# Plain fp32 router logits, fourteen weight cells of the first item fetched earlier, and sum products two down slots earlier

## What is computed

```
logits = tok @ router                       # 256 x 8, tok = rms_norm(h) * gain
top_v, top_i = top_k(logits, 2)
w = softmax(top_v)
out = sum_e gates[:, e] * ((silu(tok @ w_gate[e]) * (tok @ w_up[e])) @ w_down[e])
h = h + out;  return rms_norm(h, final_norm)
```

## Time and profile before

| | |
|---|---|
| median of three runs | 1258.49 us |
| profiled execution, span | 1259.62 us, 1257.8 us |
| PE, PEld busy | 1234.0, 872.8 us |
| DVE, ACT, POOL busy | 641.3, 562.0, 99.8 us |
| transfers | 424.48 MB, mean 337 GB/s |
| attention and dense parts | 0 to 437 us |
| first item's products | from 447 us |
| last product of an item | ends at 1248.2 us |

### The profile page before, as it was taken

The page is one execution under the profiler, slowest core; times in us unless marked ns, Lnnn a source line. Parts: engine busy times, 40 slices in busy tenths (PEclk is TensorE's granted clock), DMA queues, the critical chain, the costliest instruction groups (busy, mean ns, idle before and its releaser), DMA issues.

```text
span 1257.8 us, 18674 instructions
## 1 busy us (share of the span) xinstructions
PE 1234.0 (98%) x7266; PEld 872.8 (69%) x7266; DVE 641.3 (51%) x788; ACT 562.0 (45%) x895; POOL 99.8 (8%) x260
## 2 busy tenths in 40 slices
PE   9998999999999999999999999999999999999887
PEld 8988999999999954487575457848447765733232
DVE  5787765555765400288383257838126855620011
ACT  6565454443655421388173158527027835500001
POOL 1000000000000074100001200000210000021000
PEclk9999999999999999999999999999999999999999
DMA  9933545357632299999999999999999999999997
GB/s 329 378 136 135 182 167 188 134 166 234 228 118 100 96 426 428 422 424 427 426 426 427 424 425 426 425 426 425 428 422 426 427 407 418 424 429 424 427 427 291
DMA packets 72136, 424.48 MB, mean 337 GB/s; under 512 B 5457, under 2 KB 24050, under 8 KB 48242
## 3 DMA queue, kind: packets, MB, share of 16 engines
q1 hardware_dynamic: 71696, 422.76, 83.0%
q10 hardware_dynamic: 354, 0.54, 0.1%
HBM read 422.23 MB, written 1.05 MB: 337 GB/s over the span
## 4 chain that ended last, share of the span: by engine, by line
PE 89%; DMA 5%; ACT 2%; DVE 2%; issue 1%; POOLq 0%; POOL 0%; ACTq 0%; DVEq 0%; SPq 0%
PE psB L2100 10%; PE psY L2115 9%; PE psA L2100 7%; PE psY L1725 7%; PE psY L1727 7%; PE psY L1726 7%; PE psB L1725 6%; PE psA L1725 5%; PE psB L1727 5%; PE psB L1726 5%; PE psA L1727 5%; PE psA L1726 5%; DMA ring<-in_moe_w_up 2%; DMA ring<-in_moe_w_down 2%; PE psY L2066 1%; PE psY L1873 1%
## 5 line engine op out<-in xcount | busy, mean ns | idle before, releaser
L1585 DVE TENSOR_TENSOR wlo<-ring,whi 128x2048 fp32r<-128x2048 f32 (+3 forms) x171 | 289.1, 1727 | 150.7 <-ACT whi L950 148.5
L950 ACT CAST whi<-ring 128x1024 fp32r<-128x1024 f32 (+1 forms) x276 | 259.5, 981 | 155.1 <-DMA ring<-in_moe_w_down 72.4
L1332 DVE TENSOR_TENSOR wlo<-ring,whi 128x1024 fp32r<-128x1024 f32 (+2 forms) x104 | 152.3, 1485 | 17.6 <-ACT whi L764 17.5
L764 ACT CAST whi<-ring 128x1024 fp32r<-128x1024 f32 (+1 forms) x134 | 133.4, 1023 | 60.0 <-PE psY L1727 28.3
L2100 PE MATMUL psB<-ring,resT 128*64 128x512 f32 x620 | 149.0, 598 | 7.4 <-DMA ring<-in_moe_w_up 5.4
L2100 PE MATMUL psA<-ring,resT 128*64 128x512 f32 (+1 forms) x624 | 113.9, 486 | 0.0
L1725 PE MATMUL psA<-xhi,whi 128*128 128x256 f32 x368 | 105.0, 285 | 2.6 <-DVE wlo L1332 1.2
L2100 PEld LDWEIGHTS psA<-ring,resT 128*64 128x64 f32 x624 | 44.8, 137 | 89.1 <-issue 89.1
L1725 PE MATMUL psB<-xhi,whi 128*128 128x256 f32 x368 | 106.4, 289 | 0.0
L1726 PE MATMUL psA<-xlo,whi 128*128 128x256 f32 x368 | 102.7, 279 | 0.0
L1726 PE MATMUL psB<-xlo,whi 128*128 128x256 f32 x368 | 102.7, 279 | 0.0
(11 more groups left out here) (382 smaller groups left out, 2147.1 us busy)
## 6 DMA issues: line engine op xcount, KB each, us to landing
ring<-in_moe_w_down SPq DMA_DIRECT2D x50, 2048.0 KB, 15.6
ring<-in_moe_w_up SPq DMA_DIRECT2D x53, 1792.0 KB, 18.1
ring<-in_moe_w_gate SPq DMA_DIRECT2D x50, 1792.0 KB, 14.9
ring<-in_moe_w_gate SPq DMA_DIRECT2D x13, 1024.0 KB, 15.5
ring<-in_ffn_w_gate SPq DMA_DIRECT2D x5, 2048.0 KB, 8.8
ring<-in_ffn_w_up SPq DMA_DIRECT2D x5, 2048.0 KB, 7.8
ring<-in_ffn_w_down SPq DMA_DIRECT2D x5, 2048.0 KB, 8.0
ring<-in_moe_w_gate SPq DMA_DIRECT2D x13, 768.0 KB, 14.0
```

The source lines that it names most:

```text
L764: nc.scalar.copy(hi_of(m, size), part_of(ring, s, g, size)).then_inc(hi_done, size)
L950: nc.scalar.copy(hi_of(NG + m, size), item_part(ring, m, size)).then_inc(hi_done, size)
L1332: nc.vector.tensor_tensor(part_of(wlo, s, g, size), part_of(ring, s, g, size), f(hi_of(m, size)), ALU.subtract).then_inc(lo_done, size)
L1585: nc.vector.tensor_tensor(item_part(wlo, m, size), item_part(ring, m, size), f(hi_of(NG + m, size)), ALU.subtract).then_inc(lo_done, size)
```

## The change

The logits are multiplied in plain fp32 from `resT` (stationary, 128 x 128) with the 8 router columns moving, straight into 128 tokens x 8; the rounded parts, their copy and the summing products go. `ahead[1]` now takes the first eight spare cells, `ahead[0]` the next eight. Gate 6 of the first item is split in six cells, which wait for NG - 8 used cells only, and its last cell, which waits for NG. Between them SP waits for the last weighing of values and issues up 0 and the first cell of up 1 (eight cells). In the loop's item three down slots come in pieces, and the sums' products stand before down 1, 2 and 3 instead of 3, 4 and 5.

```diff
-    SUM_AT = {item_slot["up", 7]: (0, 1), item_slot["down", 3]: (1, 1), item_slot["down", 4]: (0, 0), item_slot["down", 5]: (1, 0)}
+    SUM_AT = {item_slot["up", 7]: (0, 1), item_slot["down", 1]: (1, 0), item_slot["down", 2]: (0, 0), item_slot["down", 3]: (1, 1)}
+    IN_PIECES = 3
...
+                last_dense = isinstance(i, int) and i == 0 and x == CELLS - GS
-                if runs and runs[-1][0] == what and runs[-1][1] + runs[-1][2] == at:
+                if runs and runs[-1][0] == what and runs[-1][1] + runs[-1][2] == at and not last_dense:
...
-            return [([ring_all, ahead[0], ahead[1]][what][:, at * W:(at + n) * W], q, n) for what, at, n, q in runs]
-        def few_used(j):
-            end = item_from[j] + item_cells[j]
+            return [([ring_all, ahead[1], ahead[0]][what][:, at * W:(at + n) * W], q, n) for what, at, n, q in runs]
+        def first_used(j, q, n):
+            end = item_from[j] + q + n
             if end <= CELLS:
                 return NG - CELLS + -(-end // GS) * GS
             return NG + max(end - CELLS - AHEAD_CELLS if end < 2 * CELLS + AHEAD_CELLS else end - CELLS, 0)
...
-                    if first:
-                        sp.wait_ge(group_used, few_used(j))
-                        if item_from[j] <= CELLS + GS < item_from[j] + item_cells[j]:
-                            sp.wait_ge(logit_mm, 1)
...
+                            if first and early_ahead(j, q):
+                                continue
+                            if first and item_from[j] + q == CELLS - GS:
+                                sp.wait_ge(pv_done, 2 * UNITS)
+                                first_rows(item_slot["up", 0], 0)
+                                first_rows(item_slot["up", 1], 0)
+                            if first:
+                                sp.wait_ge(group_used, first_used(j, q, n))
                             sp.dma_start(to, w[0][e, at * P:(at + 1) * P, q * W:(q + n) * W]).then_inc(item_full[j], 16)
...
-                    if not isinstance(i, int) and j >= FS - 2:
+                    if not isinstance(i, int) and j >= FS - IN_PIECES:
...
             split_to(NG)
-            for q in range(2):
-                act.wait_ge(block_added, 2 * q + 2)
-                raw_hi(2 * q, 2)
-            act.wait_ge(block_added, 6)
-            raw_hi(4, 2)
-            for k in range(6, KD):
-                act.wait_ge(block_added, k + 1)
-                raw_hi(k, 1)
             row_square(0, 0)
-            act.wait_ge(logit_mm, 1)
-            nc.scalar.copy(logitT[:, :], psA[0:2 * E, 0, 0:T]).then_inc(logitT_out, 1)
...
-            for q in range(2):
-                raw_lo(2 * q, 2)
...
-            dve.wait_ge(logit_mm, 2)
+            dve.wait_ge(logit_mm, 1)
...
-                    pe.wait_ge(tlo_done, k + 1)
-                    for which in (0, 1):
-                        ins = mm(psA[0:2 * E, 0, 0:T], rt_parts[:, k, :], T_part(which, k, 1),
-                                 start=k == 0 and which == 0, stop=k == KD - 1 and which == 1)
+                    pe.wait_ge(block_added, max(k + 1, 4))
+                    for tb in range(TB):
+                        ins = mm(psA[:, 1, tb * E:(tb + 1) * E], resT[:, k, tb * P:(tb + 1) * P], rt[:, k, :],
+                                 start=k == tb == 0, stop=k == KD - 1, skip_group_check=True)
...
-            pe.wait_ge(scales_set, 3)
-            pe.wait_ge(logitT_out, 1)
-            for tb in range(TB):
-                ins = mm(psA[:, 1, tb * E:(tb + 1) * E], logitT[:, tb * P:(tb + 1) * P], sum_parts[:, :], start=True, stop=True)
-            ins.then_inc(logit_mm, 1)
```

More of the change, by code:

```diff
@@ L273, in trunk @@
         pickT = sb("pickT", [P, T], F32R)
-        sum_parts = sb("sum_parts", [2 * E, E])
         rs_of_slot = sb("rs_of_slot", [P, 1])
         ident_r = sb("ident_r", [P, P], F32R)
-        rt_parts = sb("rt_parts", [P, KD, 2 * E], F32R)
         top = sb("top", [P, TB, E])
         top_at = sb("top_at", [P, TB, E], U32)
-        logitT = sb("logitT", [2 * E, T])
         count = pickT[:, :].rearrange("p (a t) -> p a t", a=2)
@@ L332, in trunk @@
         first_full = [[sem(f"first_full{j}_{a}") for a in range(len(FIRST_PARTS[j]) - 1)] for j in range(2)]
-        piece_full = [[sem(f"piece_full{a}_{k}") for k in range(FBW - 1)] for a in range(2)]
+        piece_full = [[sem(f"piece_full{a}_{k}") for k in range(FBW - 1)] for a in range(IN_PIECES)]
         item_full = [sem(f"item_full{j}") for j in range(FS)]
@@ L383, in trunk @@
         rt_gained = sem("rt_gained")
-        rt_split = sem("rt_split")
         block_done = sem("block_done")
         block_added = sem("block_added")
-        thi_done = sem("thi_done")
-        tlo_done = sem("tlo_done")
         rowT_mm = sem("rowT_mm")
@@ L392, in trunk @@
         logit_mm = sem("logit_mm")
-        logitT_out = sem("logitT_out")
         count_set = sem("count_set")
@@ L451, in blocks @@
             return t[:, first:first + n, :].rearrange("p k t -> p (k t)")
-        def T_part(which, first, n):
-            return blocks(hid_parts(first // 4)[which], first % 4, n)
         def f(ap):
@@ L701, in few_down, with early_ahead, first_rows @@
                 return moe_w_down[0][e, first:first + BANKS[b], :].rearrange("(p g) n -> p (g n)", p=P)
+            def early_ahead(j, q):
+                return CELLS <= item_from[j] + q < CELLS + GS
+            def first_rows(j, a):
+                to, q, n = few_runs(0, j)[a]
+                k = item_slots[j][1]
+                sp.dma_start(to, moe_w_up[0][0, k * P:(k + 1) * P, q * W:(q + n) * W]).then_inc(item_full[j], 16)
             def few_item(i, e, slots_of):
@@ L706, in few_item @@
                     first = isinstance(i, int) and i == 0
-                    if first:
-                        sp.wait_ge(group_used, few_used(j))
-                        if item_from[j] <= CELLS + GS < item_from[j] + item_cells[j]:
-                            sp.wait_ge(logit_mm, 1)
-                    else:
+                    if first and kind == "down":
+                        sp.wait_ge(group_used, first_used(j, 0, GS))
+                    elif not first:
                         sp.reg_add(used_past, used_past, item_cells[j])
@@ L719, in few_item @@
                     dst = few_runs(i, j)[0][0]
-                    if not isinstance(i, int) and j >= FS - 2:
+                    if not isinstance(i, int) and j >= FS - IN_PIECES:
                         for a, (b, half, g) in enumerate(DOWN_ROWS[at]):
                             sp.dma_start(dst[:, a * D:(a + 1) * D], few_down(e, b, half)[:, g * D:(g + 1) * D]).then_inc(
-                                piece_full[j - FS + 2][a] if a < FBW - 1 else item_full[j], 16)
+                                piece_full[j - FS + IN_PIECES][a] if a < FBW - 1 else item_full[j], 16)
                         continue
@@ L932, in _ @@
                     normed_hi(3, q)
-            act.wait_ge(rt_gained, 1)
-            nc.scalar.copy(rt_parts[:, :, 0:E], rt[:, :, :]).then_inc(rt_split, 1)
             nc.scalar.copy(ident_r[:, :], ident[:, :])
@@ L978, in few_hidden @@
                 nc.scalar.copy(few_act[b], few_bank(b)).then_inc(m_hhi, BANK_STEP[b])
-            def raw_hi(first, n):
-                nc.scalar.copy(T_part(0, first, n), blocks(resT, first, n)).then_inc(thi_done, n)
             def row_square(half, tb):
@@ L1172, in _ @@
             tt = nc.gpsimd.tensor_tensor
-            tt(sum_parts[:, :], ident[0:2 * E, 0:E], ident[0:2 * E, E:2 * E], ALU.add).then_inc(scales_set, 1)
             pool.wait_ge(sq_done, 4 * 3 + TB)
@@ L1176, in _ @@
             pool.wait_ge(pos_set, 1)
-            pool.wait_ge(scales_set, 3)
+            pool.wait_ge(scales_set, 2)
             link(tt(key[:, :], pos[:, TB, :], tie[:, :], ALU.add))
@@ L1588, in item_halve @@
                 return done
[L1590 to L1593, removed]
             halve_to(NG)
-            dve.wait_ge(rt_split, 1)
-            nc.vector.tensor_tensor(rt_parts[:, :, E:2 * E], rt[:, :, :], f(rt_parts[:, :, 0:E]),
-                                    ALU.subtract).then_inc(rt_split, 1)
             dve.wait_ge(block_done, 1)
@@ L1609, in _ @@
                 nc.vector.tensor_tensor(r, psB[:, 1, a * T:(a + 1) * T], r, ALU.add).then_inc(block_added, 1)
-            raw_lo(4, 2)
-            for a in range(2):
-                raw_lo(6 + a, 1)
-            dve.wait_ge(logit_mm, 2)
+            dve.wait_ge(logit_mm, 1)
             for tb in range(TB):
@@ L1982, in logits @@
                 for k in range(first, last):
-                    pe.wait_ge(tlo_done, k + 1)
-                    for which in (0, 1):
-                        ins = mm(psA[0:2 * E, 0, 0:T], rt_parts[:, k, :], T_part(which, k, 1),
-                                 start=k == 0 and which == 0, stop=k == KD - 1 and which == 1)
+                    pe.wait_ge(block_added, max(k + 1, 4))
+                    for tb in range(TB):
```

(10 more changed lines are left out.)

## The result

The changed kernel takes **1265.42 us** (median of 22 runs, 1257.12 to 1268.9) against 1258.80 for the kernel before (22 runs, 1257.91 to 1259.45): ratio 1.0040, 95% interval 1.0029 to 1.0050. It is slower, by 0.4%, outside the range that I gave. (Two of twelve executions of experiment 5 and one of the kernel before beside it took 2.5 to 7 ms at a clock of 1.00 and are left out.)

What follows compares the result with a forecast made beforehand. A ring buffer was taken to tie transfers and TensorE together, tightest near 1034 us. From 1258.5 us, 2.0 (transfer) - 0.5 (later start) + 0.5 (end) gave 1256.5 us, range 1253.8 to 1260.0.

Steps and rivals of the forecast that it cites:

- the last rival: Ahead of the first item: dearer fp32 products or a clock fall make the kernel slower, 1260.1 or 1261.7 us; chance 0.08.
- The sum: Whole kernel: 2.0 (transfer) - 0.5 (later start) + 0.5 (end) = 2.0 us faster, 1256.5 us.
- the gather's row: Profile row of fp32 gather products, 64 moving columns, same stationary size: 0.113 us an instruction, used to price the logits.
- Part 1: Fourteen cells issued earlier fill the idle 429 to 437 us; of the lead won, 2.0 us reach the end.
- lead: How far the transfer stream runs ahead after a standstill near 450 us: 4.6 us kept of 8.6.
- the tie: Near 1034 us TensorE's release of ring cells sets when a down transfer is issued, limiting the gain to 2.0 us.
- The lone transfer's 7.7: Landing time in us of 2048 KB issued with the queue empty at 327.4, expected for the transfer at 1034.2.
- a sign: Rates below 426 GB/s already ahead of all three big items' down slots, around 615, 824 and 1034 us.
- The last piece: At the kernel's end: the last transferred piece lands near 1245 us, products ending 1 us behind it.
- Part 2: Plain fp32 logits ahead of the first item: two instructions a product, 0.113 us each; first item starts 0.5 us later.
- paid in full: TensorE has no slack from 447 to 1172 us, so the first item's 0.5 us later start reaches the end whole.
- Part 3: Near the end: moved sums' products and a third pieced down slot gain 0.5 us, bounds 0 and 0.7.

Runs made afterwards that it cites:

- experiment 5: The run also called mixed: the changed kernel with two row transposes behind each pair of narrow logits products; 1263.96 us.
- wide: Changed kernel with the router's 8 columns read sixteen times over as a 128-column moving operand; 1257.81 us, ratio 0.9994 to the kernel before.
- wide_logits_only: Kernel before with only the fp32 logits, widened to 128 moving columns; no early cells, end as before; 1258.83 us, ratio 1.0000.
- end_only: Kernel before with only the moved sums' products and three pieced down slots; 1258.08 us, ratio 0.9997.
- swapped: Changed kernel with the logits' operands exchanged: 8 router columns stationary, 256 token columns moving; 1259.38 us, ratio 1.0008 to the kernel before.
- less_first: Changed kernel with widened logits, the first item's seven down slots transferred only by half; 1258.32 us, ratio 0.9999 to the kernel before.
- less_seventh: Changed kernel with widened logits, the seventh item's seven down slots transferred only by half; 1254.83 us, ratio 0.9972 to the kernel before.
- experiments 6 and 7: Experiment 6 is wide (1257.81 us); experiment 7 is the pair wide_logits_only (1258.83 us) and end_only (1258.08 us).
- mixed: Changed kernel with two row transposes behind each pair of narrow logits products, instead of sixteen in three lots; 1263.96 us, ratio 1.0034 to the kernel before.
- the disturbed execution: A second profiled execution of the changed kernel, no edit, in which the clock fell; 1266.80 us, mean clock 0.992.

## Why the prediction was wrong, step by step

**The step that failed** is the fall of the granted clock in the last rival, "A fall of the granted clock would act in the same place", with "Against it: the gather's instructions, of the same stationary size, run at 0.113", in a case with a chance of 0.08. The sum gave it nothing. It acts in just that place, in 18 of 22 runs of the result by their times, and in three of the four profiles of kernels with narrow products in blocks. The argument against it answered another question: the gather's row tells what one instruction takes, and the narrow ones take no more (0.107 us), but it says nothing of the clock. I took the clock's 1.00 "in all stretches of work" as a sign that work keeps it there. The trace before has no stretch of 3 us of fp32 products with 8 moving columns (its longest is the five counting products, 0.6 us), so its clock column could not speak for one; that was a reason for a larger chance, not for a small one. The rival's times, 1260.1 and 1261.7, lie among those of the short fall (1260.05 to 1262.23), but by luck: they were worked out from dearer instructions, and these came at the price forecast. For the fall itself the rival named the doubling ("a slot would take 6 us in place of 3") but gave no duration: 17.2 us at half clock leave 8.6 us of work undone, and 1258.5 + 8.6 = 1267.1, less what the other parts gain.

**Part 1, right in its first half.** The eight idle microseconds are filled. Bytes moved in 424 to 460: (397 x 13 + 336 x 23) - (128 x 13 + 391 x 23) = 2.2 MB more than before, 5.2 us of lead (forecast 4.6), after a hole behind 445 us (253 and 265 GB/s in 445 to 450 and 450 to 455). (128 and 391 are the rates before in 424 to 437 and 437 to 460, 397 that of the changed kernel in the first.)

**Part 1, wrong in what the tie takes.** The forecast kept 2.0 us: a landing after 7.7 in place of 9.7 us. Measured in the changed kernel, at the same transfer:

```profile
L677 SPq DMA_DIRECT2D ring<-in_moe_w_down x1: 333/333/333, 1033.8 to 1033.8; - x1
...
DMA to landing us min/median/max: 9.6/9.6/9.6
```

It is 10.1 us in wide, 10.3 in wide_logits_only, 9.2 in end_only, 8.3 in swapped, 8.7 in less_first and 8.2 in less_seventh. Up to this transfer less_seventh does what wide does, so one landing differs by 2 us between executions, and a difference of 9.7 to 7.7 can't be read from one. The lone transfer's 7.7 is reached in none, not even where 17 us of transfers are left out ahead of it. (The 6.8 us that the prediction works out from the Trainium skill's page "DMA: Bandwidth & Descriptors" come from a fit that its section "Anatomy of one DMA" gives for the GpSimd path; SP issues this transfer.)

The term was mis-sized: 2.0 forecast, 0.4 by the differences of experiments 6 and 7. With 2.0 and the other two as measured, wide would be 2.0 - 0.2 + 0.6 = 2.4 us faster than the kernel before; its interval allows at most 1.8, and that of less_first, with 17 us more of lead, at most 1.3. The rates agree, and they show the lead going elsewhere than forecast: at the down slots of the first two big items, which the prediction named as a sign but took nothing for. In the changed kernel's first profile:

```profile
460.00:500.00 40.00, 40.00 (x226) 17.54 (x224) 2.64 (x4) 5.28 (x9) 25.79 (x51) 1.00 1.00 422
...
600.00:615.00 15.00, 15.00 (x72) 9.16 (x72) 8.27 (x9) 1.28 (x2) 0.00 (x0) 1.00 1.00 418
615.00:640.00 25.00, 25.00 (x128) 11.84 (x125) 9.26 (x6) 9.99 (x11) 0.00 (x0) 1.00 0.99 407
800.00:825.00 25.00, 25.00 (x116) 16.91 (x115) 15.97 (x15) 8.41 (x9) 0.00 (x0) 1.00 0.98 405
825.00:850.00 25.00, 25.00 (x131) 12.23 (x128) 9.81 (x6) 10.00 (x11) 0.00 (x0) 1.00 0.99 411
```

Before, these five moved 427, 428, 428, 424 and 426 GB/s. The missing bytes: 0.20 + 0.15 + 0.53 + 0.48 + 0.38 = 1.7 MB, 4.1 us of the 5.2. From 1030 to 1045, at the tie on which the forecast hung, only another 0.1 MB is missing. The last piece was to land near 1245 us; it lands at 1246.5, as before.

**Part 2's size** was near: +0.3 us to the first item for +0.5, two instructions a product, 0.107 us each for 0.113. That a later start is "paid in full" isn't shown: wide_logits_only has the same path within 0.1 us and a ratio of 1.0000, within an interval of 1.1 us to each side.

**Part 3** came as forecast: 0.5, and 0.6 in end_only, though within an interval of 1.1 us to each side, which holds 0; the profile is the better witness. The last piece lands at 1246.5 in both profiled executions, and the last product of an item ends at 1239.59 + 8.04 = 1247.63 us where it was 1248.21, with 1247.5 forecast; it now waits for that piece, as forecast, as the chain of waits of the changed kernel shows:

```profile
1229.59 0.33 SPq L728
...
1230.11 16.41 DMA ring<-in_moe_w_down
1246.52 0.04 issue
1246.56 1.10 PE psY L2087 x4
```

**The sum without the fall.** With the terms as measured: 0.4 - 0.2 + 0.6 = 0.8 us faster. That this is wide's gain is no check, since the 0.4 was taken from it. The forecast of 1256.5 is 1.3 us from wide's 1257.81, where the clock doesn't fall, and 8.9 from the changed kernel.

## What to carry to other kernels

Price a product not only by its duration: where it replaces wide ones on the path, ask what its stretch may do to TensorE's clock, which the profile of the kernel before can't show, and give that its own chance and its whole price (time at half clock, halved, if the engine has no slack). Where narrow operands are all that there is, read them repeatedly into a wide moving operand: it cost 0.1 us here and saved 7.6 against the narrow form, though against the kernel before no gain is shown. And look at more than one profiled execution when the run times fall into groups: the first one of the changed kernel held nothing of its loss.

## What the runs showed of the hardware

- TensorE's granted clock fell from 2.4 to 1.2 GHz in most executions and not in all, 3 to 4 us after the first of the fp32 products with 128 x 128 stationary and 8 moving columns (three profiles), with the engine busy 6.00 of 6.00 us around it; in mixed 6.2 us after it, behind a wait of 0.79 us. It came back after about 3.5, 14 or 17 us. With 128 moving columns in the same products none of four profiles has a fall and none of 40 runs of four kernels stands apart; with 8 stationary and 256 moving columns none of 11.
- The Trainium skill's page "TensorE: Matmul & The Clock Gate", section "What's actually happening", describes the half clock as the state of an engine that is idle or has just begun. The rows here differ: TensorE was busy 23.47 of the 24.00 us ahead of the fall (416 to 440 us of the disturbed execution).
- An fp32 product with 128 x 128 stationary is two instructions, and they follow each other after 0.107 us at 8 moving columns and 0.112 at 128 (1.79 us over 16), so the columns up to there cost next to nothing; at 256 (with 8 stationary columns) it is 0.228.
